# Matmuls over 768 tokens as two of 384 columns, each in its own PSUM bank, instead of one of 512 and one of 256

## The chip, the cores and the metric

The kernel runs on one core of a Trainium2 chip. The metric is the device time of one execution in microseconds; lower is better. Several runs are given by their median.

## What is computed

Two layers of a diffusion backbone over 512 latent tokens and 256 context tokens, model width 1024, all in fp32. The reference, cut to its frame:

```python
for i in range(DEPTH):                     # DEPTH = 2
    a_lat, a_ctx = h * (1 + sc1) + sh1, hc * (1 + csc1) + csh1
    y, yc = attn_mixer(...) if i % 2 == 0 else gla_mixer(...)
    h = layer_norm(DEEPNORM_ALPHA * h + g1 * y, ...)
    f = conv_ffn(h * (1 + sc2) + sh2, ffn_w_up[i], ffn_conv_w[i], ffn_conv_b[i], ffn_w_down[i])
    h = layer_norm(DEEPNORM_ALPHA * h + g2 * f, ...)
    if need_ctx:                           # layer 0 only
        hc = ...                           # the same for the context, with its own modulation
return h
```

`conv_ffn` multiplies by `w_up` (1024 to 5632), runs a centred depthwise convolution of width 3 over the tokens (latent and context apart, zero at both ends of each), gates, `silu(gate) * val`, and multiplies by `w_down` (2816 to 1024). Shift, scale and gate of the modulation (`sh`, `sc`, `g`) differ between latent and context tokens.

## The kernel before

Activations lie transposed: features in the partitions, tokens in the free dimension, latent tokens in columns 0 to 511 and context tokens in 512 to 767 (`LAT` = 512, `TOK` = 768). A weight is cut into slabs of 128 output columns, each up to 8 tiles of 128 x 128. One slab makes one output tile [128 features, tokens].

Each fp32 product is made of three fp32r products: weights and activations are split into a high part (`w_hi`, `x_hi`, the rounded copy) and a low part (`w_lo`, `x_lo`, the rest), and high x high, high x low and low x high are summed in PSUM. A slab of 768 tokens therefore takes 8 tiles x 3 products x 2 matmuls, for one matmul writes at most 512 columns (one bank). `HALVES` = ((0, 512), (512, 768)) cuts them: 512 latent columns, then 256 context columns. The output lies in a PSUM tile `pm[j]` of 1024 columns, two banks, its columns 0 to 767 in one piece.

A slab goes through four queues. SyncE loads it into `raw`. ScalarE copies `w_hi` out of `raw` (L975), VectorE subtracts to get `w_lo` (L1394), both one slab ahead of use. TensorE multiplies: `slab` (L494), or `slab_high_first` (L476), `first_slabs` (L514), `first_modulated` (L535, L540) and `first_down` (L728) where a stage begins. Then ScalarE and VectorE empty the PSUM tile. With `tokens` = 512 the same functions use the first half alone; that is so for the queries and the output of the GLA part and for the whole FFN of layer 1.

How the tile is emptied depends on the stage:
- Attention inputs, and keys, values and gate rank of the GLA part: one ScalarE copy of 768 columns (L1023, L1179, L1211 and the like). Values are turned afterwards on TensorE (L801).
- FFN up: ScalarE writes `acc` = tile x middle tap + bias (L1150). VectorE adds the tile shifted by one token, with the tap before (L1720) and the tap after (L1725), latent and context apart. For each pair of slabs ScalarE applies `silu`, VectorE multiplies to `hid_f` (L1731), ScalarE and VectorE split it into `hid_hi` (L1161) and `hid_lo` (L1734). In layer 0 VectorE also computes a pair of modulation columns beside each second slab (L1418, L1420).
- FFN down and the output projections: ScalarE copies the tile times the gate into `tmp` (L1095 or L1097), one instruction for latent and one for context tokens. VectorE adds it to `h_res` (L1599). At the last slab before a layer norm, ScalarE squares, TensorE sums over the features (L571, L578) and spreads mean and deviation back (L561), and VectorE applies them (L1670, L1676).

TensorE may write a tile again when its readers have signalled `psum_free`: two tiles rotate in the attention and GLA projections, four in the FFN. On each engine the order is the program's own; no scheduler decides it. In each step of ScalarE and VectorE the split of the next weights comes ahead of the emptying of the tile.

```python
HALVES = ((0, LAT), (LAT, TOK))
for w, x in ((w_hi, hi), (w_hi, lo), (w_lo, hi)):
    for a, b in HALVES if tokens == TOK else HALVES[:1]:
        last = pe.matmul(out_p[:, a:b], w[slot][:, ks], x[:, k, a:b], ...)
```

Of the kernel before, what the change touches and what calls it, by code (L numbers as in the profile page):

```python
# [7 lines left out]
ALU = mybir.AluOpType  # L8
# [90 lines left out]
def trunk(nc, x_in, vec_in, rep_in, slabs_in, gates_in, first_in, ada_in, rope_in, band_in, eye_in, a2_in, level_in, out):  # L99
    ctx = ExitStack()  # L100
    with ctx:
# [159 lines left out]

        HALVES = ((0, LAT), (LAT, TOK))
        LEVELS = 1 + GLA_LEVELS
        BLOCK_LEVEL = 5
# [198 lines left out]
        def _(pe):  # L463
            def slab_high_first(base, u, hi, lo, tokens, tiles=KT, banks=2):

                s = base + u
                slot, out_p = s % 2, pm[s % 2] if banks == 2 else pm[u % 4]
                pe.wait_ge(sem["split_hi"], s + 1)
                pe.wait_ge(sem["psum_free"], s + 1 - banks)
                for w, xs in ((w_hi, (hi, lo)), (w_lo, (hi,))):  # L470
                    if w is w_lo:
                        pe.wait_ge(sem["split_lo"], s + 1)
                    for k in range(tiles):
                        for x in xs:
                            for a, b in HALVES if tokens == TOK else HALVES[:1]:
                                last = pe.matmul(out_p[:, a:b], w[slot][:, k * P:(k + 1) * P], x[:, k, a:b],  # L476
                                                 start=(k == 0 and w is w_hi and x is hi),
                                                 stop=(k == tiles - 1 and w is w_lo))
                last.then_inc(sem["slab_done"], 1)

            def slab(base, i, u, hi, lo, tokens, tiles=KT, ready=None, value=0, banks=2):
# [6 lines left out]
                for k in range(tiles):  # L488
# [3 lines left out]
                    for w, x in ((w_hi, hi), (w_hi, lo), (w_lo, hi)):  # L492
                        for a, b in HALVES if tokens == TOK else HALVES[:1]:
                            last = pe.matmul(out_p[:, a:b], w[slot][:, ks], x[:, k, a:b],  # L494
                                             start=(k == 0 and w is w_hi and x is hi),
                                             stop=(k == tiles - 1 and w is w_lo))
                last.then_inc(sem["slab_done"], 1)

            def first_slabs(base, hi, lo, tokens, tiles, before=None):


                for n, (k, ready, value) in enumerate(tiles):
# [8 lines left out]
                    for slot in (base % 2, (base + 1) % 2):  # L511
                        for w, x in ((w_hi, hi), (w_hi, lo), (w_lo, hi)):
                            for a, b in HALVES if tokens == TOK else HALVES[:1]:
                                last = pe.matmul(pm[slot][:, a:b], w[slot][:, ks], x[:, k, a:b],  # L514
                                                 start=(n == 0 and w is w_hi and x is hi),
                                                 stop=(n == KT - 1 and w is w_lo))
# [7 lines left out]
            def first_modulated(base, c, tokens):  # L524

                lag = 2 if tokens == TOK else 3
                out_of = (lambda slot: pm[slot ^ base % 2]) if base != S_GLA else (lambda slot: pm[slot])
                halves = HALVES if tokens == TOK else HALVES[:1]
                pe.wait_ge(sem["split_lo"], base + 2)
                pe.wait_ge(sem["psum_free"], base)  # L530

                def high(slot, k):
                    for w in (w_hi, w_lo):
                        for a, b in halves:
                            pe.matmul(out_of(slot)[:, a:b], w[slot][:, k * P:(k + 1) * P], x_hi[:, k, a:b],  # L535
                                      start=(k == 0 and w is w_hi), stop=False)

                def low(slot, k):
                    for a, b in halves:
                        last = pe.matmul(out_of(slot)[:, a:b], w_hi[slot][:, k * P:(k + 1) * P], x_lo[:, k, a:b],  # L540
                                         start=False, stop=(k == KT - 1))
# [179 lines left out]
            def first_down(s, tokens, tiles, hidden):  # L721

                def tile(j, k):
                    slot = (s + j) % 2
                    ks = slice(k * P, (k + 1) * P)
                    for w, x in ((w_hi, hid_hi), (w_hi, hid_lo), (w_lo, hid_hi)):
                        for a, b in HALVES if tokens == TOK else HALVES[:1]:
                            last = pe.matmul(pm[j][:, a:b], w[slot][:, ks], x[:, k, a:b],  # L728
                                             start=(k == 0 and w is w_hi and x is hid_hi),
# [226 lines left out]
        def _(act):  # L956
# [123 lines left out]
            def residual_phase(base, layer, part, tokens, norm=None, after=None):  # L1080
# [5 lines left out]
                def evacuate(s, i, u, src):  # L1086
                    n = i * 4 + u
                    done = first_res[0] + n - 1
                    if not (isinstance(done, int) and done < 1):
                        act.wait_ge(sem["residual"], done)  # L1090
                    halves = HALVES if tokens == TOK else HALVES[:1]
                    for c, (a, b) in enumerate(halves):
                        gate = mods[:, layer, bass.ds(part + n, 1), c]
                        if after is None:
                            last = act.activation(tmp[:, u % 2, a:b], src[:, a:b], ACT.Copy, scale=gate)  # L1095
                        else:
                            last = act.activation(tmp[:, u % 2, a:b], src[:, a:b], ACT.Identity, scale=gate,  # L1097
                                                  bias=scaled_ln[:, after, 1, bass.ds(n, 1)])
# [36 lines left out]
            def ffn(base, layer, tokens):  # L1135
                s0 = base
                done = FT * layer
                for g, tiles in enumerate(FF_GROUPS):
                    for part in ([range(1), act.Fori(1, tiles // 2)] if g == 0 else [act.Fori(0, tiles // 2)]):
                      with nullcontext(0) if isinstance(part, range) else part as i:  # L1140
                        for u in range(4):
                            def evacuate(s, i, u, src):
# [6 lines left out]
                                act.wait_ge(sem["acc_free"], pair + 1)  # L1149
                                act.activation(acc[:, 0:tokens], src[:, 0:tokens], ACT.Identity,  # L1150
                                               bias=vec[:, bass.ds(VEC["conv_b"] + 2 * FT * layer + tile, 1)],
# [21 lines left out]
            def take_low(s, i, u, src):  # L1173
                act.activation(low[0:2 * GLA_RANK, :], src[0:2 * GLA_RANK, 0:TOK], ACT.Copy).then_inc(sem["psum_free"], 1)
                act.wait_ge(sem["psum_free"], s + 1)
                act.sem_inc(sem["low_done"], 1)

            def take_key(s, i, u, src):
                act.activation(gla_k[:, u - 1, :], src[:, 0:TOK], ACT.Copy).then_inc(sem["psum_free"], 1)  # L1179

# [26 lines left out]
            for i in range(2):  # L1207
                def take_value(s, i, u, src):

                    act.wait_ge(sem["v_turned"], TOK // P + u - 1 + 4 * i)  # L1210
                    act.activation(v_turn[:, u % 2, :], src[:, 0:TOK], ACT.Copy).then_inc(sem["psum_free"], 1)  # L1211

# [175 lines left out]
        def _(dve):  # L1388
# [302 lines left out]
            def ffn(base, layer, tokens):  # L1691
                s0 = base
                done = FT * layer
                for g, tiles in enumerate(FF_GROUPS):
# [10 lines left out]
                    with nullcontext(0) if unrolled else dve.Fori(0, tiles // 2) as i0:  # L1705
                      for i in range(tiles // 2) if unrolled else (i0,):
                        if not unrolled:
                            order.enter(i, 4 + per)
                        for u in range(4):
                            def evacuate(s, i, u, src):  # L1710
# [6 lines left out]
                                dve.wait_ge(sem["lin_done"], 2 * pair + u % 2 + 1)  # L1717
                                halves = HALVES if tokens == TOK else HALVES[:1]
                                for a, b in halves:
# [4 lines left out]
                                for a, b in halves:  # L1724
# [395 lines left out]
```

## Time and profile before

| | us |
|---|---|
| median of 3 runs | 1724.87 |
| the runs | 1719.32 to 1728.21 |
| profiled execution, its own time | 1721.16 |
| its span, first to last instruction | 1719.4 |
| TensorE busy | 1657.0 (96%) |
| VectorE busy | 1112.6 (65%) |
| ScalarE busy | 712.4 (41%) |
| mean granted TensorE clock | 0.989 |

The profile is of one execution. The span is what the trace covers; the execution's time is 1.8 us longer. Busy shares are of the span. The ends of matmuls are modelled and overlap, so the cost of a matmul in a dense stretch is read from the distance between starts or from a whole stretch, and not from its recorded duration.

### The profile page before, as it was taken

How to read it: one execution, taken by the hardware profiler on the slowest of the kernel's cores; microseconds unless marked ns; L12 is line 12 of the kernel's file. 1: busy time of each engine (PE TensorE's matmuls, PEld its weight loads, DVE VectorE, ACT ScalarE, POOL GpSimd, SP SyncE). 2: the span in 40 equal slices, each digit the busy share in tenths (PEclk: the TensorE clock that was granted, in tenths of full speed). 3: DMA queues.
4: the chain of work that ended last, by engine and by line, in shares of the span. 5: the costliest groups of instructions: out<-in, count | busy, mean ns of one | idle time of the engine just before them, and what ended most of it. 6: DMA issues, size and time to landing. Idle time of an engine off the chain costs nothing.

```text
span 1719.4 us, 23804 instructions
## 1 busy us (share of the span) xinstructions
PE 1657.0 (96%) x9008; PEld 1389.7 (81%) x9008; DVE 1112.6 (65%) x1728; ACT 712.4 (41%) x1060; POOL 85.9 (5%) x57
## 2 busy tenths in 40 slices
PE   7999999998999999999999899999989999999997
PEld 6888877887888888888888777867777788888885
DVE  6678666476887578865766645187845664564456
ACT  4212665336333233322334664256644543343345
POOL 0200000122000000000002200000002100000002
PEclk9999999999999999999999999999999999999999
DMA  9344100031334333343322121010112233333332
GB/s 361 116 148 152 57 1 1 25 135 37 136 109 147 135 110 133 111 146 136 110 61 89 33 67 59 27 36 26 37 62 87 73 98 98 98 97 93 95 93 74
DMA packets 37279, 159.50 MB, mean 93 GB/s; under 512 B 4145, under 2 KB 4401, under 8 KB 31057
## 3 DMA queue, kind: packets, MB, share of 16 engines
q1 hardware_dynamic: 37202, 158.44, 27.5%
q8 instruction: 52, 0.85, 0.2%
q14 instruction: 25, 0.20, 0.0%
HBM read 156.33 MB, written 2.10 MB: 92 GB/s over the span
## 4 chain that ended last, share of the span: by engine, by line
PE 86%; DVE 6%; ACT 4%; issue 2%; DMA 1%; SPq 0%; POOL 0%; ACTq 0%; DVEq 0%
PE pm L494 60%; PE pm L476 5%; PE pm L728 4%; PE pm L648 3%; PE pm L514 2%; PE pm L674 2%; PE pm L908 2%; PE pm L661 1%; ACT mod_t L994 1%; DMA ada_w<-first_ada 1%; PE pm L851 1%; DVE sides L1818 1%; DVE h_res L1670 1%; PE pm L832 1%; PE pm L605 1%
## 5 line engine op out<-in xcount | busy, mean ns | idle before, releaser
L1394 DVE TENSOR_TENSOR w_lo<-raw,w_hi 128x1024 fp32r<-128x1024 f32 x185 | 231.0, 1250 | 357.4 <-ACT w_hi L975 354.7
L975 ACT ACTIVATE w_hi<-raw 128x1024 fp32r<-128x1024 f32 x181 | 191.8, 1060 | 621.5 <-PE pm L494 527.0
L494 PE MATMUL pm<-x_hi,w_hi 128*128 128x512 f32 (+1 forms) x1464 | 424.1, 351 | 0.0
L494 PE MATMUL pm<-x_hi,w_lo 128*128 128x512 f32 (+1 forms) x1464 | 423.2, 350 | 0.0
L494 PE MATMUL pm<-x_lo,w_hi 128*128 128x512 f32 (+1 forms) x1464 | 422.4, 350 | 0.0
L494 PEld LDWEIGHTS pm<-x_hi,w_hi 128*128 128x128 f32 x1464 | 236.1, 188 | 39.6 <-DVE w_lo L1394 0.7
L494 PEld LDWEIGHTS pm<-x_hi,w_lo 128*128 128x128 f32 x1464 | 235.8, 188 | 38.5
L494 PEld LDWEIGHTS pm<-x_lo,w_hi 128*128 128x128 f32 x1464 | 235.7, 188 | 38.5
L1420 DVE CUSTOM_DVE_ANT_0 ada_w<-ada_w,cond_rep 128x1024 f32<-128x1024 f32 x80 | 102.5, 1281 | 0.0
L494 PE MATMUL pm<-hid_hi,w_hi 128*128 128x512 f32 x330 | 98.9, 354 | 0.3 <-DVE w_lo L1394 0.3
L494 PE MATMUL pm<-hid_lo,w_hi 128*128 128x512 f32 x330 | 98.8, 353 | 0.0
L494 PE MATMUL pm<-hid_hi,w_lo 128*128 128x512 f32 x330 | 98.8, 353 | 0.0
L1974 POOL TENSOR_TENSOR sum<-sum,sq_t 128x768 f32<-128x768 f32 (+1 forms) x28 | 46.9, 1674 | 937.2 <-ACT sq_t L1105 937.2
L1161 ACT ACTIVATE hid_hi<-hid_f 128x768 f32 (+3 forms) x44 | 32.6, 741 | 124.6 <-DVE hid_f L1731 124.6
L1418 DVE CUSTOM_DVE_ANT_0 junk_f<-ada_w,cond_rep 128x1024 f32<-128x1024 f32 x56 | 68.3, 1219 | 0.0
L1734 DVE TENSOR_TENSOR hid_lo<-hid_f,hid_hi 128x512 f32 (+2 forms) x44 | 36.3, 826 | 44.7 <-ACT hid_hi L1161 44.7
L494 PEld LDWEIGHTS pm<-hid_hi,w_hi 128*128 128x128 f32 x330 | 54.0, 188 | 9.7 <-DVE w_lo L1394 0.7
L494 PEld LDWEIGHTS pm<-hid_hi,w_lo 128*128 128x128 f32 x330 | 54.0, 188 | 9.1
L494 PEld LDWEIGHTS pm<-hid_lo,w_hi 128*128 128x128 f32 x330 | 54.0, 188 | 9.0
L908 PE MATMUL pm<-x_sum,raw 128*128 128x512 f32 x128 | 59.3, 593 | 0.0
L648 PE MATMUL pm<-qkv 128*128 128x256 f32 (+3 forms) x176 | 55.3, 419 | 2.1 <-ACT probs_t L1041 1.1
L674 PE MATMUL pm<-probs_t,v_tok 128*128 128x128 f32 x400 | 54.0, 279 | 1.5 <-DVE x_lo L1529 0.7
(242 smaller groups left out, 2512.8 us busy)
## 6 DMA issues: line engine op xcount, KB each, us to landing
raw<-slabs SPq DMA_DIRECT2D x185, 512.0 KB, 3.6
ada_w<-ada SPq DMA_DIRECT2D x44, 1024.0 KB, 4.9
ada_w<-first_ada SPq DMA_DIRECT2D x4, 1024.0 KB, 18.6
raw<-gates SPq DMA_DIRECT2D x8, 512.0 KB, 3.5
h_res<-x SPq DMA_DIRECT2D x4, 768.0 KB, 16.6
out<-h_res SPq DMA_DIRECT2D x8, 256.0 KB, 2.0
rope<-rope SPq DMA_DIRECT2D x1, 512.0 KB, 21.6
level_f<-level SPq DMA_DIRECT2D x1, 448.0 KB, 3.2
```

Source lines behind the costliest of these rows:

```text
L476: last = pe.matmul(out_p[:, a:b], w[slot][:, k * P:(k + 1) * P], x[:, k, a:b], start=(k == 0 and w is w_hi and x is hi), stop=(k == tiles ...
L494: last = pe.matmul(out_p[:, a:b], w[slot][:, ks], x[:, k, a:b], start=(k == 0 and w is w_hi and x is hi), stop=(k == tiles - 1 and w is w_lo))
L648: last = pe.matmul(pm[n % 3][:, at:at + b - a], q, qkv[:, u["k"], a:b], start=True, stop=(u["band"] is None or at > 0))
L674: last = pe.matmul(weighed(n), v_tok[:, t, u["v"] * P:(u["v"] + 1) * P], probs_t[:, n % 2, j * P:(j + 1) * P], start=(j == 0), stop=(j == ...
L728: last = pe.matmul(pm[j][:, a:b], w[slot][:, ks], x[:, k, a:b], start=(k == 0 and w is w_hi and x is hid_hi), stop=(k == tiles - 1 and w i ...
L908: last = pe.matmul(gate_bank, gate_raw(i)[:, k * P:(k + 1) * P], x_sum[k][:, :], start=(k == 0), stop=(k == KT - 1))
L975: act.activation(w_hi[nxt % 2][:, :], raw[nxt % 4][:, :], ACT.Copy).then_inc(sem["split_hi"], 1)
L1394: dve.tensor_tensor(w_lo[nxt % 2][:, :], raw[nxt % 4][:, :], w_hi[nxt % 2][:, :].bitcast(FP32), ALU.subtract).then_inc(sem["split_lo"], 1)
L1418: junk_written = order.mark(dve.tensor_tensor_reduce(junk[:, :], w, cond_rep[:, 0, :], 1.0, 0.0, ALU.mult, ALU.add, to[:, half, 0:1]))
L1420: last = dve.tensor_tensor_reduce(w, w, cond_rep[:, 1, :], 1.0, 0.0, ALU.mult, ALU.add, to[:, half, 1:2])
L1734: dve.tensor_tensor(hid_lo[:, bass.ds(2 * i + u // 2, 1), 0:tokens].rearrange("p a b -> p (a b)"), hid_f[:, 0:tokens], hid_hi[:, bass.ds(2 ...
L1974: pool.tensor_tensor(sum2[:, 0:tokens], sum2[:, 0:tokens], sq_t[:, n % 2, 0:tokens], ALU.add).then_inc(sem["summed"], 1)
```

## The change

`pieces` replaces `HALVES` in all products: columns 0 to 383 of the tokens go to columns 0 to 383 of the PSUM tile (its first bank), tokens 384 to 767 to columns 512 to 895 (its second bank). The readers of the tile follow. Where one instruction read 768 columns it now reads a view of 2 x 384. Where latent and context tokens are treated apart (gates, convolution), `by_kind` gives three pieces: latent 0 to 383, latent 384 to 511, context 512 to 767. The convolution's shifted reads stop or start one column short only at the real ends of a kind. The logits of the GLA part keep 512 and 256.

```diff
+        HALF = TOK // 2
+        def pieces(tokens):
+            return ((0, 0, HALF), (512, HALF, TOK)) if tokens == TOK else ((0, 0, LAT),)
+        def by_kind(tokens):
+            return ((0, 0, 0, HALF), (0, 512, HALF, LAT), (1, 512 + LAT - HALF, LAT, TOK)) if tokens == TOK else ((0, 0, 0, LAT),)
+        def bank_of(src, tokens=TOK):
+            return src[:, 0:LAT] if tokens == LAT else src.rearrange("p (a b) -> p a b", b=512)[:, :, 0:HALF]
+        def tile_for(v, tokens=TOK):
+            return v if tokens == LAT else v.rearrange("p (a b) -> p a b", b=HALF)
...
-                        for a, b in HALVES if tokens == TOK else HALVES[:1]:
-                            last = pe.matmul(out_p[:, a:b], w[slot][:, ks], x[:, k, a:b],
+                        for at, a, b in pieces(tokens):
+                            last = pe.matmul(out_p[:, at:at + b - a], w[slot][:, ks], x[:, k, a:b],
...
-                act.activation(qkv[:, s, :], src[:, 0:TOK], ACT.Copy).then_inc(sem["psum_free"], 1)
+                act.activation(tile_for(qkv[:, bass.ds(s, 1), :].rearrange("p a b -> p (a b)")), bank_of(src), ACT.Copy).then_inc(sem["psum_free"], 1)
...
-                    for c, (a, b) in enumerate(halves):
+                    for c, at, a, b in by_kind(tokens):
                         gate = mods[:, layer, bass.ds(part + n, 1), c]
                         if after is None:
-                            last = act.activation(tmp[:, u % 2, a:b], src[:, a:b], ACT.Copy, scale=gate)
+                            last = act.activation(tmp[:, u % 2, a:b], src[:, at:at + b - a], ACT.Copy, scale=gate)
...
-                                for a, b in halves:
-                                    last = dve.scalar_tensor_tensor(acc[:, a + 1:b], src[:, a:b - 1], before, acc[:, a + 1:b],
-                                                                    ALU.mult, ALU.add)
+                                ends = (LAT, TOK)
+                                for _, at, a, b in by_kind(tokens):
+                                    n = b - a - (b in ends)
+                                    last = dve.scalar_tensor_tensor(acc[:, a + 1:a + 1 + n], src[:, at:at + n], before,
+                                                                    acc[:, a + 1:a + 1 + n], ALU.mult, ALU.add)
...
-                                for a, b in halves:
-                                    last = dve.scalar_tensor_tensor(acc[:, a:b - 1], src[:, a + 1:b], after, acc[:, a:b - 1],
-                                                                    ALU.mult, ALU.add)
+                                for _, at, a, b in by_kind(tokens):
+                                    skip = int(a in (0, LAT))
+                                    last = dve.scalar_tensor_tensor(acc[:, a + skip - 1:b - 1], src[:, at + skip:at + b - a], after,
+                                                                    acc[:, a + skip - 1:b - 1], ALU.mult, ALU.add)
```

The lines of the new program are 16 to 18 higher than those before (L494 becomes L512, L1095 becomes L1111, L1720 becomes L1737).

TensorE, attention inputs, at the end of the third slab and the start of the fourth (`w_hi_59` and `w_lo_61` are the weights of odd slabs, `square_a` the squares of a head). Before:

```order
L476 MATMUL pm<-x_hi,w_lo_60 128x512
L476 MATMUL pm<-x_hi,w_lo_60 128x256
L623 MATMUL pm<-ones,square_a 128x1 x6
L494 MATMUL pm<-x_hi,w_hi_59 128x512
L494 MATMUL pm<-x_hi,w_hi_59 128x256
L494 MATMUL pm<-x_lo,w_hi_59 128x512
L494 MATMUL pm<-x_lo,w_hi_59 128x256
```

and now:

```order
L494 MATMUL pm<-x_hi,w_hi_58 128x384 x2
L494 MATMUL pm<-x_lo,w_hi_58 128x384 x2
L494 MATMUL pm<-x_hi,w_lo_60 128x384 x16
L640 MATMUL pm<-ones,square_a 128x1 x6
L512 MATMUL pm<-x_hi,w_hi_59 128x384 x2
L512 MATMUL pm<-x_lo,w_hi_59 128x384 x2
L512 MATMUL pm<-x_hi,w_lo_61 128x384 x2
```

The order of products is kept; each pair of 512 and 256 columns is one row of two equal matmuls.

ScalarE, the start of the output projection of attention, first slab. Before:

```order
L975 ACTIVATE w_hi_58<-raw_56 128x1024
L1095 ACTIVATE tmp<-pm,mods 128x512
L1095 ACTIVATE tmp<-pm,mods 128x256
L1105 ACTIVATE sq_t<-h_res 128x768
L975 ACTIVATE w_hi_59<-raw_57 128x1024
```

and now:

```order
L992 ACTIVATE w_hi_58<-raw_56 128x1024
L1111 ACTIVATE tmp<-pm,mods 128x384
L1111 ACTIVATE tmp<-pm,mods 128x128
L1111 ACTIVATE tmp<-pm,mods 128x256
L1121 ACTIVATE sq_t<-h_res 128x768
L992 ACTIVATE w_hi_59<-raw_57 128x1024
```

One instruction more stands between the split of the weights and the square that follows the residual.

VectorE, the first up slab of a loop turn in layer 0's FFN (rows named ISA work out addresses and waits). Before:

```order
L1394 TENSOR_TENSOR w_lo_60<-raw_56,w_hi_58 128x1024
L1717 ISA
L1720 ISA
L1720 SCALAR_TENSOR_TENSOR acc_g<-pm,vec,acc_g 128x511
L1720 SCALAR_TENSOR_TENSOR acc_g<-pm,vec,acc_g 128x255
L89 ISA
L1725 ISA
L1725 SCALAR_TENSOR_TENSOR acc_g<-pm,vec,acc_g 128x511
L1725 SCALAR_TENSOR_TENSOR acc_g<-pm,vec,acc_g 128x255
```

and now:

```order
L1410 TENSOR_TENSOR w_lo_60<-raw_56,w_hi_58 128x1024
L1733 ISA
L1737 ISA
L1737 SCALAR_TENSOR_TENSOR acc_g<-pm,vec,acc_g 128x384
L1737 SCALAR_TENSOR_TENSOR acc_g<-pm,vec,acc_g 128x127
L1737 SCALAR_TENSOR_TENSOR acc_g<-pm,vec,acc_g 128x255
L89 ISA
L1743 ISA
L1743 SCALAR_TENSOR_TENSOR acc_g<-pm,vec,acc_g 128x383
L1743 SCALAR_TENSOR_TENSOR acc_g<-pm,vec,acc_g 128x128
L1743 SCALAR_TENSOR_TENSOR acc_g<-pm,vec,acc_g 128x255
```

Each of the two taps has one piece more, and the elements add up to the same 766.

## Rows read from the trace of the kernel before

**Rows 1.** The page: span, busy time, TensorE clock in 40 slices, chain by engine.

```profile
span 1719.4 us, 23804 instructions
...
PE 1657.0 (96%) x9008; PEld 1389.7 (81%) x9008; DVE 1112.6 (65%) x1728; ACT 712.4 (41%) x1060; POOL 85.9 (5%) x57
...
PEclk9999999999999999999999999999999999999999
...
PE 86%; DVE 6%; ACT 4%; issue 2%; DMA 1%; SPq 0%; POOL 0%; ACTq 0%; DVEq 0%
```

**Rows 2.** The chain in order of time: start us, duration us, what (FFN stages).

```profile
560.69 174.72 PE pm L494 x1008
...
1438.65 5.44 PE pm L476 x24
```

**Rows 3.** Groups by form: shapes, count, busy us, mean ns, idle before; TensorE, L494.

```profile
L494 PEld LDWEIGHTS pm<-x_hi,w_hi 128*128 128x128 f32 x1464 | 236.1, 188 | 39.6 <-DVE w_lo L1394 0.7 <-issue 0.6
...
L494 PE MATMUL pm<-x_lo,w_hi 128*128 128x256 f32 x552 | 153.3, 278 | 0.0
```

**Rows 4.** Timeline of TensorE in a down stage: start us, span us, form, count.

```profile
599.71 0.51 PE L494 MATMUL pm<-hid_hi,w_lo 128*128 128x512 f32 x2
...
599.94 0.27 PE L494 MATMUL pm<-hid_hi,w_lo 128*128 128x256 f32 x1
```

**Rows 5.** Timeline of TensorE in the attention scores, plain fp32.

```profile
177.56 0.59 PE L648 MATMUL pm<-qkv 128*128 128x256 f32 x2
177.99 0.38 PE L653 MATMUL pm<-band,eye 128*128 128x128 f32 x2
...
183.94 0.81 PE L648 MATMUL pm<-qkv 128*128 128x384 f32 x2
184.59 0.61 PE L653 MATMUL pm<-band,eye 128*128 128x128 f32 x4
```

**Rows 6.** The chain in order of time: transposes of 128 columns, plain fp32.

```profile
181.49 2.62 PE pm L691 x24
```

**Rows 7.** Groups by form: VectorE, the convolution's first tap.

```profile
L1720 DVE SCALAR_TENSOR_TENSOR acc_g<-pm,vec,acc_g 128x511 f32<-128x511 f32 x44 | 32.7, 744 | 0.0
...
L1720 DVE SCALAR_TENSOR_TENSOR acc_g<-pm,vec,acc_g 128x255 f32<-128x255 f32 x22 | 10.4, 474 | 0.0
```

**Rows 8.** Timeline of VectorE and ScalarE in an up stage with modulation pairs.

```profile
649.26 1.23 DVE L1394 TENSOR_TENSOR w_lo<-raw,w_hi 128x1024 fp32r<-128x1024 f32 x1 [0.39 <-issue]
650.40 1.14 DVE L1720 SCALAR_TENSOR_TENSOR acc_g<-pm,vec,acc_g 128x511 f32<-128x511 f32 x2
...
652.25 1.06 ACT L975 ACTIVATE w_hi<-raw 128x1024 fp32r<-128x1024 f32 x1 [6.29 <-PE pm L494]
```

**Rows 9.** Groups by form: ScalarE, the gated copy of a residual tile.

```profile
L1095 ACT ACTIVATE tmp<-pm,mods 128x512 f32<-128x512 f32 x40 | 26.9, 672 | 7.4 <-PE pm L494 7.4
...
L1095 ACT ACTIVATE tmp<-pm,mods 128x256 f32<-128x256 f32 x24 | 11.2, 466 | 0.0
```

**Rows 10.** Timeline of ScalarE and TensorE at the start of the output projection.

```profile
332.78 1.03 ACT L1095 ACTIVATE tmp<-pm,mods 128x512 f32<-128x512 f32 x2
...
333.96 0.59 PE L476 MATMUL pm<-x_hi,w_hi 128*128 128x512 f32 x2 [1.19 <-ACT tmp L1095]
```

**Rows 11.** Timeline of TensorE after the fourth value slab of the GLA part.

```profile
1089.80 0.87 PE L801 MATMUL pm<-eye,v_turn 128*128 128x128 f32 x6 [1.27 <-ACT v_turn L1211]
```

**Rows 12.** The chain in order of time, end of the output projection.

```profile
385.12 1.06 ACT tmp L1095 x2
```

**Rows 13.** Timeline of VectorE and TensorE at the second layer norm.

```profile
957.07 0.17 DVE L1655 TENSOR_TENSOR small<-pm,stat_a 128x6 f32<-128x6 f32 x1
...
957.29 2.39 PE L561 MATMUL pm<-eye,small 128*128 128x128 f32 x19
```

**Rows 14.** The chain and VectorE's timeline, end of layer 0's last up stage.

```profile
901.81 12.48 PE pm L728 x72
...
908.41 0.96 DVE L1734 TENSOR_TENSOR hid_lo<-hid_f,hid_hi 128x768 fp32r<-128x768 f32 x1 [1.02 <-ACT hid_hi L1161]
```

More of the change, by code:

```diff
@@ L474, in slab_high_first @@
                         for x in xs:
-                            for a, b in HALVES if tokens == TOK else HALVES[:1]:
-                                last = pe.matmul(out_p[:, a:b], w[slot][:, k * P:(k + 1) * P], x[:, k, a:b],
+                            for at, a, b in pieces(tokens):
+                                last = pe.matmul(out_p[:, at:at + b - a], w[slot][:, k * P:(k + 1) * P], x[:, k, a:b],
                                                  start=(k == 0 and w is w_hi and x is hi),
@@ L492, in slab @@
                     for w, x in ((w_hi, hi), (w_hi, lo), (w_lo, hi)):
-                        for a, b in HALVES if tokens == TOK else HALVES[:1]:
-                            last = pe.matmul(out_p[:, a:b], w[slot][:, ks], x[:, k, a:b],
+                        for at, a, b in pieces(tokens):
+                            last = pe.matmul(out_p[:, at:at + b - a], w[slot][:, ks], x[:, k, a:b],
                                              start=(k == 0 and w is w_hi and x is hi),
@@ L512, in first_slabs @@
                         for w, x in ((w_hi, hi), (w_hi, lo), (w_lo, hi)):
-                            for a, b in HALVES if tokens == TOK else HALVES[:1]:
-                                last = pe.matmul(pm[slot][:, a:b], w[slot][:, ks], x[:, k, a:b],
+                            for at, a, b in pieces(tokens):
+                                last = pe.matmul(pm[slot][:, at:at + b - a], w[slot][:, ks], x[:, k, a:b],
                                                  start=(n == 0 and w is w_hi and x is hi),
@@ L527, in first_modulated @@
                 out_of = (lambda slot: pm[slot ^ base % 2]) if base != S_GLA else (lambda slot: pm[slot])
-                halves = HALVES if tokens == TOK else HALVES[:1]
                 pe.wait_ge(sem["split_lo"], base + 2)
@@ L533, in high @@
                     for w in (w_hi, w_lo):
-                        for a, b in halves:
-                            pe.matmul(out_of(slot)[:, a:b], w[slot][:, k * P:(k + 1) * P], x_hi[:, k, a:b],
+                        for at, a, b in pieces(tokens):
+                            pe.matmul(out_of(slot)[:, at:at + b - a], w[slot][:, k * P:(k + 1) * P], x_hi[:, k, a:b],
                                       start=(k == 0 and w is w_hi), stop=False)
                 def low(slot, k):
-                    for a, b in halves:
-                        last = pe.matmul(out_of(slot)[:, a:b], w_hi[slot][:, k * P:(k + 1) * P], x_lo[:, k, a:b],
+                    for at, a, b in pieces(tokens):
+                        last = pe.matmul(out_of(slot)[:, at:at + b - a], w_hi[slot][:, k * P:(k + 1) * P], x_lo[:, k, a:b],
                                          start=False, stop=(k == KT - 1))
@@ L726, in tile @@
                     for w, x in ((w_hi, hid_hi), (w_hi, hid_lo), (w_lo, hid_hi)):
-                        for a, b in HALVES if tokens == TOK else HALVES[:1]:
-                            last = pe.matmul(pm[j][:, a:b], w[slot][:, ks], x[:, k, a:b],
+                        for at, a, b in pieces(tokens):
+                            last = pe.matmul(pm[j][:, at:at + b - a], w[slot][:, ks], x[:, k, a:b],
                                              start=(k == 0 and w is w_hi and x is hid_hi),
```

14 lines of the change are left out of this document (5 added, 9 removed).

## The prediction

> **What bounds the kernel now.** I read the page first. TensorE is busy 96% of a span of 1719.4 us, at full granted clock in every slice, VectorE 65%, ScalarE 41%, and the chain of work that ended last runs through TensorE for 86% of the span [rows 1]. So the question is what one product costs on TensorE, and only then what the other engines do at the few joints of the chain.
>
> The chain in order of time gives that cost over long unbroken stretches. In the down and up products of layer 0, with 768 tokens, 1008 matmuls take 174.72 us [rows 2]. They are 504 pairs (512 columns, then 256, with the same weights), so a pair takes 174.72 / 504 = 346.7 ns. In layer 1 the same code runs 512 tokens only: 24 matmuls take 5.44 us, 226.7 ns each [rows 2]. The difference, 120.0 ns, is the 256-column one. The timeline has the same split: a pair starts at 599.71, its 256 columns at 599.94 [rows 4]. The clock is 2.4 GHz there (granted clock full, rows 1), so the columns alone would be 213.3 and 106.7 ns. What is left over is 13.3 ns for the long matmul and 13.3 ns for the short one: a fixed part per matmul, plus the columns. The "mean ns" of a group (278 ns for the 256-column one [rows 3]) is a latency that overlaps its neighbours and prices nothing here. The profile records one weight load for each matmul, 1464 of either in this group, also where the weights stay the same [rows 3].
>
> **The change, part by part.**
>
> *TensorE.* 105 slabs have 768 tokens: 16 attention inputs, 8 outputs, 44 up, 24 down, and 13 of the GLA part; 97 of them have 8 tiles and 8 have 6. With three products a tile that is 3 x (97 x 8 + 8 x 6) = 2472 pairs, or 857 us, half of the span. The change leaves the number of matmuls, of weight loads and of columns alone and makes 512 + 256 into 384 + 384. With 13.3 ns and the columns, 384 columns take 160 + 13.3 = 173.3 ns and the pair 346.7 ns: a difference of nothing.
>
> No fp32r product of 384 columns is in the trace, so this needs bounds. The one row with 384 columns is a plain fp32 score product of attention, which goes as two matmuls of two passes each: 183.94 to 184.59, 0.65 us for the two, 325 ns each [rows 5]. The 256-column ones beside it take 177.56 to 177.99, 215 ns each [rows 5], and a chain of 24 of 128 columns takes 2.62 us, 109 ns each [rows 6]. From 109 and 215 a straight line gives 321 at 384; measured are 325, and the starts are read to 10 ns. Nothing happens at 384 that the neighbours don't show. Lower end: if the excess of the long matmul grows with its columns instead of being fixed (226.7 x 384/512 = 170 ns), the pair takes 340 ns and 2472 pairs save 16.5 us. Upper end: one pass of the plain product lies about 2 ns above the straight line, and the time of a start is read to 10 ns over four passes, 2.5 ns; 2.5 ns on each of 4944 matmuls is +12.4 us. I take 0, since two lengths out of two leave exactly the same 13.3 ns.
>
> The Trainium skill (TensorE: Matmul & The Clock Gate, "Back-to-back issue gap") gives N/2.4 + 2.5 ns for a warm matmul. For 512 columns that is 215.8 ns, and the trace has 226.7, so the measurement decides; by the page's rule the pair would be 325.0 ns in either form and the sum zero as well.
>
> *VectorE.* The convolution reads PSUM twice per up slab, in two pieces each; now it takes three, since the 384 boundary cuts inside the latent tokens. That is 2 more instructions for each of 44 slabs, 88 in all, with the same elements. A 511-column piece is recorded at 744 ns and a 255-column one at 474 [rows 7], so a column costs 1.055 ns. Two of them together span 1.14 us [rows 8], so the first holds the engine 1.14 - 0.474 = 0.67 us; its columns are 0.54, and 0.13 us is the price of one more instruction. 88 x 0.13 = 11.4 us more on VectorE, beside TensorE's work. The cover is thinnest where the modulation pairs run in between: there the split of the next weights (L1394) starts at 649.26 and is done at 650.49, and TensorE ends the slab before it at about 652.2, when the next split starts on ScalarE (652.25) [rows 8]. The slack is 1.7 us; two more pieces ahead of that split take 0.26. The other wait on this work is at the end of the last up stage, where TensorE has 8 tile products of 1.04 us before it needs the last hidden tile: from 901.81 to 910.13, and the tile is done at 909.37 [rows 14]. Of 0.76 us, 0.26 go. Cost: 0. Without that cover it would be 0.26 us per pair of slabs, 22 x 0.26 = 5.7 us.
>
> *ScalarE.* A residual tile of 768 tokens is copied with a gate per kind of token: two instructions, now three (384, 128, 256), 32 more in all. 512 columns are recorded at 672 ns, 256 at 466 [rows 9]: 0.805 ns a column. The two span 1.03 us [rows 10], so the first holds 0.56, of which 0.41 are columns: 0.15 us for one more. It is on the chain at three joints only:
> - At the start of the output projection TensorE waits 1.19 us for this copy and starts at 333.96 [rows 10]. +0.15.
> - At its end the copy of the last tile is in the chain, from 385.12 [rows 12], and the statistics behind it follow. +0.15.
> - At the end of layer 0's down products TensorE has its own sums first. VectorE's mean is ready at 957.24, TensorE gets to it at 957.29 [rows 13]: slack 0.05 us, so +0.10.
>
> In the middle of the stages four banks rotate, and nothing waits. Layer 1's FFN has 512 tokens and does not change.
>
> The other copies (qkv, keys, values, the convolution's first term) stay one instruction of 768 elements, now read as 2 x 384 across two banks. The price lies between nothing and one instruction's fixed part, 0.15 us; it tells where TensorE waits for it: once at the first qkv tile and twice at the value tiles, one of them with 1.27 us idle [rows 11]. That is 0 to 0.45 us. I take 0, since the engine walks the same number of elements in one instruction.
>
> *Sum:* 0 + 0 + 0.15 + 0.15 + 0.10 = +0.4 us on the profiled execution of 1721.16 us (span 1719.4 and 1.8 around it), 1721.6. The median of the runs shown, 1724.87, lies 3.7 us above that execution, and the three runs are 8.9 us apart. I put the difference on the median: **1725.3 us**. A measurement of this kernel can tell about 0.5%, 8.6 us, from no change.
>
> **The rivals.**
>
> *A: the weight load binds the short matmul.* While 256 columns stream, the weights of the next matmul are loaded. The load is recorded at 188 ns [rows 3], more than the 120 ns between starts. If 120 ns is the load's floor and not 106.7 + 13.3, and the long matmul's excess goes with its columns, each 384 has room to hide its load and costs 170 ns: 340 a pair, -16.5 us, 1708.8 us, 1% faster. For it: 188 is over 120, and 226.7 is also 17/16 of 213.3. Against it: 24 plain matmuls with their own loads start every 109 ns [rows 6], so a load does not need 120; and the two excesses would be equal by accident. Chance 0.10. The Trainium skill (the same page, "LDWEIGHTS") puts a load at columns / 1.2, an estimate of 107 ns for 128 columns, which speaks for a load that fits under the 120.
>
> *B, the other side: a matmul of 384 columns has a larger fixed part.* The place is every pair of the 105 slabs, the price 2.5 ns a matmul: +12.4 us and the 0.4 above, 1737.7 us, 0.7% slower. It passes 0.5% from 8.2 us / 4944 = 1.7 ns a matmul on. For it: the plain 384 row lies 4 ns above the line. Against it: that is within the reading. Chance 0.07.
>
> *C: VectorE runs late.* If the two extra pieces per slab used up the 1.7 us before the split, TensorE would wait in each pair of slabs. That needs 0.87 us a piece against 0.13. At 1.0 us a piece the 22 pairs would lose 2.0 - 1.7 = 0.3 us each, 6.6 us, and the time would be about 1732 us. Chance 0.02.
>
> That the change does not do what it says is excluded: every 768-token product stands as 384 x2 in the order of TensorE.
>
> **How the numbers follow.** No difference beyond a few tenths: 0.81, at 1725.3. A 0.10, B 0.07, C 0.02. The spread of the median itself (three runs over 8.9 us) is larger than my terms and can take "no difference" to 1719 or 1731. The range from 1713 to 1734 holds that case with its own scatter and the smaller half of A's and B's sizes; it leaves out the full -16.5 us and the full +12.4 us. Faster by over 0.5%: 0.11 (A and a little scatter). Within 0.5%: 0.79. Slower by over 0.5%: 0.10 (B, C and a little scatter).
>
> **What would show it.** In the stretch that answers to rows 2, 504 products should again take 174.7 us, with starts 173 ns apart instead of 230 and 120. The 1008 matmuls there in 171.4 us would be A, in 177.2 us B. The 256-wide form on L494's successor is gone and one of 384 stands in its place, with weight loads still one each. The convolution groups show three forms of about 610, 340 and 474 ns, so that 610 + 340 ns stand for 744 and VectorE is busy longer by 88 x 0.2 = 18 us as recorded, with overlapping ends counted; the idle time before the split of the weights shrinks by some 11 us. The gated copy of the residual spans about 1.18 us instead of 1.03. A wait of TensorE for VectorE inside the up stages would be C and make the forecast wrong, as would any stretch of 768-token products whose pair is not 347 ns.

## The result, and the profile after

| | before | after |
|---|---|---|
| median, 20 runs each | 1726.21 us | 1716.29 us |
| lowest to highest | 1716.57 to 1730.21 | 1713.36 to 1720.88 |
| ratio, 95% interval | | 0.9947 (0.9933 to 0.9960) |
| profiled execution, its own time | 1721.16 us | 1718.99 us |
| its span | 1719.4 us | 1717.1 us |

The change is 0.53% faster, 9.9 us by the medians. The forecast was no difference. 1716.3 lies inside its range of 1713 to 1734, but by luck: the low end was made of scatter and half of rival A's size, and neither is what happened. The gain was missed. The two profiled executions are only 2.3 us apart. The rest of the gain is not in this pair of traces at all, which is the first thing to explain.

The page of the changed kernel, the lines that answer to [rows 1]:

```profile
span 1717.1 us, 23924 instructions
...
PE 1654.5 (96%) x9008; PEld 1497.8 (87%) x9008; DVE 1124.2 (65%) x1816; ACT 718.0 (42%) x1092; POOL 85.8 (5%) x57
...
PEclk9999999999999999999999999999989999999999
...
PE 86%; DVE 6%; ACT 4%; issue 2%; DMA 1%; POOL 0%; SPq 0%; ACTq 0%; DVEq 0%
```

The number of matmuls and weight loads is the same (9008 each), VectorE has 88 instructions more and ScalarE 32, as counted. The chain in order of time (start, duration, what) at the stages of 768 tokens; L494, L512 and L745 are what L476, L494 and L728 were:

```profile
333.38 8.56 PE pm L494 x48
341.95 41.62 PE pm L512 x240
...
551.01 8.32 PE pm L494 x48
559.33 174.72 PE pm L512 x1008
...
995.97 8.32 PE pm L512 x48
```

The 1008 matmuls of the FFN take 174.72 us in both traces [rows 2]. The 240 of the output projection take 41.62. The same stretches of the trace before, which the prediction does not use:

```profile
333.96 8.72 PE pm L476 x48
342.68 42.42 PE pm L494 x240
...
552.37 8.32 PE pm L476 x48
...
998.85 8.48 PE pm L494 x48
```

42.42 us for 120 pairs is 353.5 ns a pair, not 346.7: already in this trace the output projection and single slabs of the GLA part (8.48 us against 8.32) ran at another pace than the FFN, at a granted clock of 1.00. Each tile of three pairs takes 1.06 us there instead of 1.04. After the change no long stage does.

The other terms, on ScalarE and VectorE:

```profile
332.06 1.18 ACT L1111 ACTIVATE tmp<-pm,mods 128x384 f32<-128x384 f32 x3
...
333.38 0.59 PE L494 MATMUL pm<-x_hi,w_hi 128*128 128x384 f32 x2 [1.33 <-ACT tmp L1111]
...
648.90 1.26 DVE L1737 SCALAR_TENSOR_TENSOR acc_g<-pm,vec,acc_g 128x384 f32<-128x384 f32 x3
...
1086.04 0.87 PE L818 MATMUL pm<-eye,v_turn 128*128 128x128 f32 x6 [1.27 <-ACT v_turn L1227]
```

The gated copy spans 1.18 us, before 1.03 [rows 10], and TensorE waits 1.33 us for it, before 1.19. The convolution's pieces span 1.26 us, before 1.14 [rows 8]. TensorE's wait for the copy of the values through the two-bank view is 1.27 us as before [rows 11].

### The profile page after: what moved, and what is told of

Its sections match the earlier page's. It is cut to its first block, busy times and chain, and to the rows that moved or that the text cites. A ratio compares the mean times of both kernels' runs of the same rounds, so it can differ in the third digit from the quotient of the medians.

```text
span 1717.1 us, 23924 instructions
## 1 busy us (share of the span) xinstructions
PE 1654.5 (96%) x9008; PEld 1497.8 (87%) x9008; DVE 1124.2 (65%) x1816; ACT 718.0 (42%) x1092; POOL 85.8 (5%) x57
## 4 chain that ended last, share of the span: by engine, by line
PE 86%; DVE 6%; ACT 4%; issue 2%; DMA 1%; POOL 0%; SPq 0%; ACTq 0%; DVEq 0%
PE pm L512 60%; PE pm L494 5%; PE pm L745 4%; PE pm L665 3%; PE pm L532 2%; PE pm L691 2%; PE pm L925 2%; PE pm L678 1%; ACT mod_t L1011 1%; DMA ada_w<-first_ada 1%; PE pm L868 1%; DVE sides L1836 1%; DVE h_res L1686 1%; PE pm L849 1%; PE pm L622 1%
## 5 line engine op out<-in xcount | busy, mean ns | idle before, releaser
L512 PE MATMUL pm<-x_hi,w_hi 128*128 128x384 f32 (+1 forms) x1464 | 423.1, 350 | 0.0
L512 PE MATMUL pm<-x_hi,w_lo 128*128 128x384 f32 (+1 forms) x1464 | 421.6, 349 | 0.0
L512 PE MATMUL pm<-x_lo,w_hi 128*128 128x384 f32 (+1 forms) x1464 | 421.5, 349 | 0.0
L512 PEld LDWEIGHTS pm<-x_hi,w_hi 128*128 128x128 f32 x1464 | 267.0, 188 | 15.7 <-DVE w_lo L1410 0.7
L512 PEld LDWEIGHTS pm<-x_lo,w_hi 128*128 128x128 f32 x1464 | 267.8, 188 | 14.1
L512 PEld LDWEIGHTS pm<-x_hi,w_lo 128*128 128x128 f32 x1464 | 267.5, 188 | 14.3
L512 PE MATMUL pm<-hid_hi,w_hi 128*128 128x384 f32 (+1 forms) x330 | 98.8, 353 | 0.2 <-DVE w_lo L1410 0.2
L512 PE MATMUL pm<-hid_hi,w_lo 128*128 128x384 f32 (+1 forms) x330 | 98.7, 353 | 0.0
L512 PE MATMUL pm<-hid_lo,w_hi 128*128 128x384 f32 (+1 forms) x330 | 98.6, 353 | 0.0
L512 PEld LDWEIGHTS pm<-hid_hi,w_hi 128*128 128x128 f32 x330 | 60.4, 188 | 4.9 <-DVE w_lo L1410 0.7
L512 PEld LDWEIGHTS pm<-hid_hi,w_lo 128*128 128x128 f32 x330 | 60.4, 188 | 4.3
L512 PEld LDWEIGHTS pm<-hid_lo,w_hi 128*128 128x128 f32 x330 | 60.4, 188 | 4.2
```

The costliest lines, as they stand in the source:

```text
L512: last = pe.matmul(out_p[:, at:at + b - a], w[slot][:, ks], x[:, k, a:b], start=(k == 0 and w is w_hi and x is hi), stop=(k == tiles - 1 a ...
```

## The experiments

**Theory 1**: with 512 + 256 columns TensorE can run a dense stage in a slow rhythm, 20 ns more a tile. Which stages do so differs from execution to execution, and the FFN of layer 0 alone is worth 528 tiles x 20 ns = 10.6 us. **Theory 2**: the gain is luck in when TensorE's clock comes back after the layer norms. In the trace before, the granted clock was 0.52 from 989 to 992 us, the first 3 us of the GLA products, which is the 1.2 GHz level; in the trace after it was 1.00 there and the first slab took 8.54 us instead of 10.12. After a wait at 1285 us it was the other way round. The granted clock is a row of the profile: 1.00 is 2.4 GHz, about 0.5 is 1.2 GHz.

### The kernel before again, and the change in parts

`again` has no edit. The next three take a width of the first piece by stage (`first_of`), with the readers cut to match:

```diff
+        def first_of(base):                       # ffn_384
+            return TOK // 2 if S_FFN0 <= base < S_GLA else LAT
...
+            return LAT if S_FFN0 <= base < S_GLA else TOK // 2     # rest_384
...
+            return 448                            # all_448
+        def pieces(tokens, base):
+            n = first_of(base)
+            return ((0, 0, n), (512, n, TOK)) if tokens == TOK else ((0, 0, LAT),)
```

> The kernel before, unchanged, as a second profiled execution and as a control of the comparison. Theory 1 (slow stretches: with 512 + 256 columns TensorE can fall, after a disturbance, into a rhythm in which a tile takes 1.06 us instead of 1.04, and executions differ in how many stages run so; in the profiled one it was the output projection and part of the GLA stages, 1.9 us): ratio 1.000 within 0.2%, times spread over about 10 us again, and the profile shows tiles of 1.06 us, perhaps in other stages than before. If an execution over 1724 us is caught, the FFN of layer 0 should be slow: 528 tiles x 20 ns = 10.6 us. Theory 2 (the gain is luck in when the clock returns to full after the layer norms, 1.6 us each time): no or the same few slow tiles, and the spans differ by multiples of 1.6 us at the norms.

> 384 + 384 only in the FFN of layer 0 (68 slabs, 528 tiles), 512 + 256 elsewhere. Theory 1: the FFN can no longer run slow, so the executions over 1724 us vanish: median 8 us lower than before, ratio 0.995 to 0.996; the profile has slow tiles in the output projection or GLA stages only. Theory 2: ratio 1.000.

> 384 + 384 in the attention and GLA stages (37 slabs), 512 + 256 in the FFN of layer 0. Theory 1: 2 to 3 us lower than before (ratio 0.998 to 0.999) and the spread of about 10 us stays. Theory 2: ratio 1.000.

> 448 + 320 columns in all 105 slabs; copies of 768 columns become two instructions on ScalarE. Theory 1, if what matters is only that the shorter matmul has room for the weight load (320 columns are 133 ns): as the change, ratio 0.995, no tile of 1.06 us. If it needs two equal matmuls: as before, with slow tiles. Theory 2: ratio 1.000.

Measured: `again` 1727.66 us, ratio 0.9996 (0.9971 to 1.0021). `ffn_384` 1718.71 us, 0.9942 (0.9925 to 0.9959). `rest_384` 1727.52 us, 0.9990 (0.9971 to 1.0008). `all_448` 1717.18 us, 0.9938 (0.9917 to 0.9960). The whole effect that can be measured sits in the FFN of layer 0, as theory 1 says; theory 2 gives none of this. The profile of `ffn_384` has what theory 1 asks for: the output projection, still 512 + 256, in 42.42 us and the FFN stretch in 174.72. The 2 to 3 us expected of `rest_384` are too few for its interval to confirm or exclude. In `all_448` one expectation failed, "no tile of 1.06 us". Its FFN and output projection are at the normal pace, but in the GLA part the second slab is not (8.48 us for 24 pairs, after the change 8.32, at a granted clock of 1.00), nor is the third (14.16 us with 24 matmuls of 512 columns behind it, after the change 14.03):

```profile
998.03 8.48 PE pm L522 x48
...
1009.28 14.16 PE pm L522 x72
```

`again` also caught an execution with the FFN in the slow rhythm (its span 1725.9 us). Its chain:

```profile
341.07 42.42 PE pm L494 x240
...
426.19 110.24 PE pm L494 x624
536.42 16.96 PE pm L728 x96
553.38 8.48 PE pm L476 x48
561.87 178.08 PE pm L494 x1008
```

178.08 us for the 504 pairs of [rows 2], 353.3 ns each. And its timeline of TensorE, where three pairs take from 599.86 to 600.92, 1.06 us:

```profile
599.86 0.51 PE L494 MATMUL pm<-hid_hi,w_hi 128*128 128x512 f32 x2
600.21 0.53 PE L494 MATMUL pm<-hid_lo,w_hi 128*128 128x512 f32 x2
600.57 0.51 PE L494 MATMUL pm<-hid_hi,w_lo 128*128 128x512 f32 x2
600.92 0.51 PE L494 MATMUL pm<-hid_hi,w_hi 128*128 128x512 f32 x2
```

The granted clock is 1.00 in the 1008 matmuls of either trace, and the bytes moved by DMA are alike (123 GB/s here, 125 before). The stage is slow from its third slab (417.70) to its end (960.44), 542.7 us against 532.5 in the trace before (419.25 to 951.73): 10.3 us. It does not change in between, nor does it in any other profile: each execution has one pace for the whole FFN. The times fall into two heaps to match. Of 35 runs of the kernel before on one chip (the one of `zigzag` below), 8 lie at or below 1722.73 us and 27 at 1726.80 or above, with none between. On the three other sets of runs of this kernel the gap is narrower (1719.32 to 1724.67, 1722.97 to 1725.26, 1721.06 to 1726.59 us), and 17 of 76 runs lie below it.

### A break in the stream, other widths, other orders

```diff
+                if u == 3:                        # bump: output projection
+                    for j in range(6):
+                        pe.matmul(pm[2][:, LAT + j:LAT + j + 1], eye[:, :], ones[:, 0:1], start=True, stop=True)
...
+                        if layer == 0:            # bump: FFN, the same six
+                            bump()
                         slab_high_first(s, 2, x_hi, x_lo, tokens, banks=4)
```

> The kernel before, with six plain fp32 matmuls of one column (result unused) at two places: in the output projection ahead of its fourth slab, and in the FFN of layer 0 ahead of its third slab. Attention inputs have such matmuls between the slabs and their unrolled loop behind them ran at the normal pace (384 matmuls in 66.67 us) in all profiles of 512 + 256. If the slow rhythm is a state that TensorE carries along and that a short break in the dense stream resets: the 240 matmuls behind take 41.6 us instead of 42.42, and the FFN of layer 0 is at the normal pace in every execution: median 1719 to 1721 us (ratio 0.995 to 0.996, each break costs up to 1.2 us), no executions over 1724. If the break does not reset it: 42.4 us, and ratio 1.000 to 1.001 with the same spread.

Measured: 1730.51 us, ratio 1.0008 (0.9980 to 1.0037), only 2 of 12 runs below 1723. The second branch holds: the six matmuls reset nothing. In its profile the output projection is slow before the break (8.72 us for the slab) and right behind it, and the FFN is slow behind its own. (Between single slabs the pace can change: in the trace before, the third slab of the attention inputs takes 8.72 us, 8.56 in `again`, and the slabs behind its six matmuls are at the normal pace.)

```profile
343.36 42.52 PE pm L494 x240
...
565.59 178.08 PE pm L494 x1008
```

To see what a weight load needs by itself, `three` cuts the 256 columns into two (the first product of a slab keeps 256, since it opens the sum):

```diff
+        THIRDS = ((0, LAT), (LAT, LAT + P), (LAT + P, TOK))
-                        for a, b in HALVES if tokens == TOK else HALVES[:1]:
+                        for a, b in HALVES[:1] if tokens != TOK else HALVES if (k == 0 and w is w_hi and x is hi) else THIRDS:
```

> All 768-token products in three matmuls, 512 + 128 + 128 columns, each with its own weight load (the first product of a slab keeps 512 + 256). It gives the spacing of fp32r matmuls of 128 columns, whose columns take 53.3 ns. If a weight load has a floor that binds the 256-column matmul (113 ns from its start to the next one in a normal stretch): 128-column ones are also spaced by 107 to 113 ns, a product takes about 440 to 453 ns instead of 347, the kernel some 240 us more. If it has not: 60 to 67 ns, a product 360 ns, the kernel about 33 us more.

Measured: 1966.22 us, 245 us above the profiled execution before. The 1008 matmuls of the FFN stretch are 1491 now and take 227.78 us, against 174.72. The weight loads in its timeline (three a product, merged):

```profile
700.00 0.19 PEld L495 LDWEIGHTS pm<-hid_hi,w_lo 128*128 128x128 f32 x1
700.11 0.54 PEld L495 LDWEIGHTS pm<-hid_hi,w_hi 128*128 128x128 f32 x3
700.57 0.54 PEld L495 LDWEIGHTS pm<-hid_lo,w_hi 128*128 128x128 f32 x3
```

A product takes 454 ns on average. The loads of one start at 700.11, 700.22 and 700.46, those of the next at 700.57. Where no matmul of 512 columns stands between two loads, the second starts 108 to 112 ns after the first in 965 of 986 cases of the stretch and 115 ns after it in the rest, although 128 columns are only 53.3 ns of columns. The two matmuls of 128 columns themselves start 57 to 60 ns apart, so it is the load that keeps this distance and not the matmul. So in fp32r a weight load takes 108 to 112 ns here, and the 106.7 ns of 256 columns are a little less than that. The kernels compare as follows. The numbers are distances from the start of one matmul to the start of the next, averaged over the 1008 matmuls of the FFN stretch (the slow 448 + 320 over its slab at 998.03, the last line over 502 matmuls of layer 1):

| kernel, rhythm | after the long one | after the short one | pair |
|---|---|---|---|
| 512 + 256, normal | 231.8 ns | 114.9 ns | 346.7 |
| 512 + 256, slow (again) | 236.5 | 116.9 | 353.3 |
| 496 + 272, normal | 224.2 | 122.5 | 346.7 |
| 496 + 272, slow (again_496) | 227.9 | 125.4 | 353.3 |
| 480 + 288 | 215.9 | 132.5 | 348.3 |
| 448 + 320, normal | 203.3 | 143.3 | 346.7 |
| 448 + 320, slow | 204.3 | 149.0 | 353.3 |
| 384 + 384 | 173.3 | 173.3 | 346.7 |
| 512 alone, layer 1 | 226.7 | | |

In the normal rhythm the short matmul of the kernel before takes 112 to 118 ns, a little more than a load, and the long one 230 to 233, more than the 226.7 of a 512-column matmul among its like. The Trainium skill (TensorE: Matmul & The Clock Gate, "LDWEIGHTS") has 128 / 1.2 = 107 ns for this load, no longer than 256 columns stream; the trace shows 1 to 5 ns more, and that puts 256 columns just under it. The slow rhythm has the same pair, 353.3 ns, whatever the cut, also with 320 columns (133.3 ns), which are well over a load.

> 480 + 288 columns in all 105 slabs. 288 columns take 120 ns, 13 ns more than 256. If the slow rhythm needs a short matmul that leaves no more time than the weight load (floor about 107 to 113 ns), 120 ns are enough: no tile of 1.06 us, the output projection's 240 matmuls take 41.6 us, ratio 0.995. If more room is needed: 42.4 us there and times spread as before.

> 496 + 272 columns in all 105 slabs; 272 columns take 113.3 ns. On the edge: with a floor of 107 ns the slow rhythm is gone (41.6 us for the 240 matmuls), with 113 ns or more it is there (42.4 us).

> 496 + 272 columns again, for the share of slow executions: 3 of 10 were above 1726 us in the first job. If those are executions with a slow FFN, a profile that catches one has 1008 matmuls in about 178 us; a profile of one below 1723 has 174.7. A share between that of 256 (about three quarters above 1724) and of 288 (1 in 10) is expected: 2 to 4 in 10.

Edits: `return 480` and `return 496` in `first_of`. Measured: `all_480` 1721.29 us, ratio 0.9965 (0.9942 to 0.9989), 9 of 10 runs below 1723. Its pair is 348.3 ns in every long stage; 2472 x 1.6 ns = 4 us would account for what it loses to 384. `all_496` 1721.35 us, 0.9977 (0.9950 to 1.0005); `again_496` 1719.52 us, 0.9965 (0.9941 to 0.9988); 17 of the 22 runs of the two are below 1723. The profile of `all_496` has the output projection (41.61 us) and the FFN (174.72) normal and the attention inputs slow: 67.94 us for 384 matmuls, where the five profiles with 512 before 256 or 256 before 512 throughout have 66.67:

```profile
111.48 67.94 PE pm L522 x384
```

The profile of `again_496` caught an execution of the slow heap:

```profile
335.05 8.56 PE pm L504 x48
343.62 41.61 PE pm L522 x240
419.60 8.48 PE pm L504 x48
...
563.76 178.08 PE pm L522 x1008
```

The output projection is normal here and the FFN slow. So 272 columns do not end the slow rhythm but make it rarer in the FFN: 5 of 22 runs, against 27 of 35 with 256. That the last eight slabs of the attention inputs run slow was seen only with 272.

The last two keep 512 + 256 and all readers and change only the order:

```diff
+        def in_order(tokens):                     # short_first
+            return HALVES[::-1] if tokens == TOK else HALVES[:1]
...
+        def in_order(tokens):                     # zigzag
+            turn_[0] ^= 1
+            return (HALVES if turn_[0] else HALVES[::-1]) if tokens == TOK else HALVES[:1]
```

> 512 + 256 as before with the short matmul first in every product, so that the weights loaded while it streams are the same ones again, and new weights are loaded under the long one. If any load under a short matmul is too tight: as before, ratio 1.000, the output projection's 240 matmuls in 42.4 us. If only the load of new weights matters: 41.6 us and ratio 0.995.

> 512 + 256 as before, but the order within a product alternates: 512, 256, then 256, 512, so that two short matmuls (and two long ones) follow each other; all readers as before. If a 256-column matmul is shorter than the 110 to 114 ns that a weight load needs (measured with three matmuls a product), and the long one beside it catches that up, two short ones in a row cannot: slow tiles at least as often as before, ratio 1.000 to 1.01. If the slow rhythm comes from the strict alternation of long and short, it goes: ratio 0.995.

Measured: `short_first` 1729.06 us, ratio 1.0006 (0.9985 to 1.0027), 10 of 12 runs above 1724. `zigzag` 1720.19 us, 0.9960 (0.9940 to 0.9980), no run of 12 above 1722.3. The second is a surprise and goes against the simple form of theory 1: two short matmuls in a row give a load no more room, yet the slow rhythm never comes. Its FFN stretch and output projection:

```profile
340.85 41.81 PE pm L501 x240
...
558.96 175.56 PE pm L501 x1008
```

It is 348.3 ns a pair in every long stage of this profile. `short_first` gives a mixed answer. By its times any load under a short matmul will do, for the slow heap is as full as before. But its profiled execution, one of the fast heap (span 1714.2 us), had both stages normal, 41.61 and 174.72 us: the output projection is not bound to be slow, as it was in the four other profiles with 512 + 256 there. No profile caught it slow.

> The changed kernel again: a second profile and a control. Theory 1: ratio 0.994 to 0.996, all times below 1722, every 768-token stage at 1.04 us a tile (174.72 us for the 1008 matmuls, 41.6 for the 240). Against theory 1 would be a stage at 1.06 us a tile.

Measured: 1716.99 us, ratio 0.9942 (0.9924 to 0.9960), 12 runs from 1714.96 to 1721.25. Its 240 and 1008 matmuls take 41.62 and 174.72 us, as theory 1 expects. The first slab of its GLA part takes 10.09 us, as in the kernel before, and the profiled execution (1718.0 us) is still none of the slow heap: against theory 2.

| kernel | runs below 1723 us | from 1723 us on |
|---|---|---|
| before (512 + 256), 35 runs on one chip | 8 | 27 |
| before, the 76 runs of the other sets | 17 | 59 |
| again, short_first, rest_384, bump (FFN 512 + 256) | 10 | 37 |
| 496 + 272, both sets | 17 | 5 |
| 480 + 288 | 9 | 1 |
| 448 + 320 | 6 | 0 |
| 384 in the FFN only | 8 | 0 |
| zigzag | 12 | 0 |
| after, both sets | 32 | 0 |

A run close to 1723 us can be put in either column: a run of `bump` at 1723.65 us carries its two breaks, and all times of 480 + 288 are some 4 us up. In the fourteen profiled executions the pace of the FFN agrees with the table: 178.08 us in those with spans of 1725.9, 1728.7 and 1732.8 us (`again`, `again_496`, `bump`), 174.72 to 175.56 us in the ten others with two matmuls a product, whose spans are 1719.4 us at most; `three` stands apart. No cut or order tried here beats the changed kernel; `all_448` and `ffn_384` equal it.

## Why the prediction missed

1. **TensorE, "a difference of nothing".** In the normal rhythm it was right to the last digit: 346.7 ns a pair and 174.72 us for the stretch. The step that failed is the one before: one stretch of one execution was taken as the pace of all 2472 pairs. In the same trace the output projection ran at 353.5 ns, which the prediction's own last sign ("any stretch of 768-token products whose pair is not 347 ns") would have caught. And by the times of 27 in 35 runs the FFN runs so too, 10.3 us longer. The change takes this away, and that is the 9.9 us of the medians. The forecast put the median, 3.7 us above the profiled execution, down to scatter. It lies in the slow heap and the profiled execution in the other.
2. **"Two lengths out of two leave exactly the same 13.3 ns."** The 120.0 ns for 256 columns came from a subtraction that presumed 226.7 ns for the 512 beside it, so the equal remainders were one number used twice. Measured from starts it is 114.9 and 231.8. The single row at hand, 599.71 to 599.94, is 230 ns read to 10 ns and could not tell the two apart. The forecast of the normal pair survives because the sum is 346.7 ns for 512 + 256, 496 + 272, 448 + 320 and 384 + 384 alike; why, no run shows, and 480 + 288 differs.
3. **Rival A** (chance 0.10) had the sign, and a weight load about as long as the short matmul is what was found, but the gain has another size and form. A pair of 384 is not 340 ns; nothing is gained in the normal rhythm, the slow one is lost. That the load causes the slow rhythm is not shown. Its "against", plain loads 109 ns apart [rows 6], rules out a load of 120 ns but not one longer than 256 columns: 109 is over 106.7.
4. **Rival B** did not occur: 384 columns take 173.3 ns. **Rival C** did not either: 1.26 us for three pieces, and the split of the weights (647.76 to 648.99) still ends 1.9 us before TensorE's next slab (650.89).
5. **ScalarE, +0.4 us.** This came out. The copy is 0.15 us longer at the start and the end of the output projection (1.18 us, before 1.03; in the chain 1.21, before 1.06). At the second norm, the time from the slab's end to the spread of the mean is 5.67 us (950.41 to 956.08), before 5.58 (951.73 to 957.31): 0.09 us more, where 0.10 was forecast. The two-bank view costs nothing (qkv, values).
6. **VectorE, 0 on the path.** Two pieces of 613 and 342 ns are recorded in place of one of 744, and a tap holds the engine 0.12 us longer. That is 11.6 us of busy time more on the profile's page (1124.2, before 1112.6), the 11.4 of the working and not the 18 named among the signs. All of it is covered.

The 2.3 us between the two profiled spans are 0.8 us in the output projection, 0.16 us for its first slab and several times 0.15 in the GLA part, with 0.77 us because the first weights land earlier (the first matmul starts at 21.75 us, before at 22.52), against the +0.4. The two stretches of half clock cancel: the first GLA slab takes 8.54 us, before 10.12, and the products after the wait at 1285 us take 1.6 us more than before.

## What to carry to other kernels

When a dense stage is all there is to win, divide every long stretch of the chain by its matmul count, not one; a pace that differs between stretches of the same code is a finding. When the runs of one kernel fall into two heaps, a single profile shows one of them: profile again until both are caught. With fp32r weights reloaded for each matmul, cut the columns into equal pieces where the readers allow it: none of the 40 runs with 384 + 384 in the FFN fell into the slow heap, and no profiled stage that has it was slow. A piece of 256 columns beside one of 512 can cost 2% of the stage. 448 + 320 was as fast as 384 + 384 here, but only 6 runs of it exist, and two of its GLA slabs ran slow.

## What was not expected, and what stays open

- A rhythm of TensorE that lasts 540 us without a pause, through loops and changes of weights, and is 2% slower at the same granted clock. Six one-column matmuls, ahead of the FFN's third slab or inside the output projection, do not end it.
- The time of a weight load in fp32r, 108 to 112 ns, just over the 106.7 ns of 256 columns.
- Shown: in the FFN it occurs with 256 columns in steady alternation with 512 (with the short one first by the times alone), less with 272, and in no run with 384, with 448 + 320 (6 runs) or with the order turned in every product. Elsewhere it also came up in the attention inputs with 272 columns and in two GLA slabs with 320. Not shown: how it arises. That the load is longer than the short matmul is measured, but it is neither enough nor needed: `zigzag` keeps it and is free of the slow rhythm, and 320 columns are longer than the load and were slow in two slabs. Every slow stage had pieces of two lengths in steady alternation, which is a hint and no proof. What decides at the start of a stage which rhythm it takes was not found.
- Cutting 480 + 288 or alternating the order costs 1.6 ns a pair more than 512 + 256, 448 + 320 or 384 + 384; why was not tried.
